# Delta-rule heads: both quarters of filling of a level in front of its second product

## What is computed

```python
lower = jnp.where(strict, jnp.einsum("bhncd,bhnsd->bhncs", k_beta, k) * decay, 0.0)
t_inv = lax.linalg.triangular_solve(eye + lower, jnp.broadcast_to(eye, lower.shape),
                                    left_side=True, lower=True, unit_diagonal=True)
u = jnp.einsum("bhncs,bhnse->bhnce", t_inv, v_beta)
w = jnp.einsum("bhncs,bhnsd->bhncd", t_inv, k_beta * eg[..., None])
def step(state, xs):
    q_c, qk_c, u_c, w_c, k_c, gl = xs
    v_new = u_c - jnp.einsum("bhcd,bhde->bhce", w_c, state)
    o = jnp.einsum("bhcd,bhde->bhce", q_c, state) + jnp.einsum("bhcs,bhse->bhce", qk_c, v_new)
    state = state * jnp.exp(gl)[..., None, None] + jnp.einsum("bhcd,bhce->bhde", k_c, v_new)
    return state, o
```

## Time and profile before

| | |
|---|---|
| median of 3 runs | 2359.76 us (2343.94 to 2362.39) |
| profiled execution | 2355.82 us, span 2354.1 us |
| TensorE busy | 2219.3 us, 94% of the span |
| VectorE, ScalarE, GpSimd busy | 57%, 36%, 24% |
| chain that ended last | TensorE 75%, VectorE 15%, issue 4%, ScalarE 2%, DMA 2% |
| heads 0 to 7 | about 100 to 720 us, 78.3 to 78.4 us for each of the heads in the middle |

### The profile page before, as it was taken

One profiled execution on the slowest core, in us unless ns is written; L12 is line 12 of the kernel. 1 busy time (PEld: TensorE's weight loads), 2 busy tenths in 40 slices (PEclk: granted clock), 3 DMA queues, 4 the chain that ended last, 5 costly groups with the idle time before them and its releaser, 6 DMA issues.

```text
span 2354.1 us, 31041 instructions
## 1 busy us (share of the span) xinstructions
PE 2219.3 (94%) x10792; PEld 1831.5 (78%) x10792; DVE 1335.0 (57%) x1845; ACT 847.9 (36%) x1239; POOL 561.8 (24%) x584
## 2 busy tenths in 40 slices
PE   5899999999979999999999999999899999999997
PEld 5687878787867877888888788888666677888886
DVE  6667656765663445343356655554577776655531
ACT  1323222322222223223223545432456554554422
POOL 3277667766770012000011000001000000000021
PEclk6899999999999999999999999999999999999999
DMA  6233333333322322333333233333211112333332
GB/s 223 81 99 90 92 94 98 91 92 94 98 81 72 98 87 84 98 96 92 93 95 99 80 98 98 98 90 98 63 54 54 52 48 86 101 98 98 92 92 67
DMA packets 355154, 212.78 MB, mean 90 GB/s; under 512 B 8536, under 2 KB 342802, under 8 KB 354963
## 3 DMA queue, kind: packets, MB, share of 16 engines
q1 hardware_dynamic: 346346, 185.82, 27.1%
q0 software_dynamic: 7680, 25.17, 3.5%
q10 hardware_dynamic: 1065, 0.96, 0.1%
HBM read 209.82 MB, written 2.10 MB: 90 GB/s over the span
## 4 chain that ended last, share of the span: by engine, by line
PE 75%; DVE 15%; issue 4%; ACT 2%; DMA 2%; DVEq 0%; ACTq 0%; POOL 0%; POOLq 0%; SPq 0%
PE ps L1970 22%; PE ps L1972 22%; PE ps L1971 22%; PE ps L2140 3%; PE ps L1997 2%; DVE w_lo L1155 2%; DMA raw<-diff_w_qkv 1%; DVE small L1854 1%; DVE small L1485 1%; DVE gd_y_t L1459 1%; DVE a_sb L1883 1%; DVE gd_q_s L1346 1%; ACT at_swap L1059 1%; DVE gd_q_g L1447 1%; PE ps L2089 1%
## 5 line engine op out<-in xcount | busy, mean ns | idle before, releaser
L1970 PE MATMUL ps<-h_hi,w_hi 128*128 128x512 f32 x1896 | 776.3, 409 | 33.8 <-DVE gd_y_t L1459 8.9
L1972 PE MATMUL ps<-h_hi,w_lo 128*128 128x512 f32 x1896 | 750.7, 396 | 0.0
L1971 PE MATMUL ps<-h_lo,w_hi 128*128 128x512 f32 x1896 | 750.1, 396 | 0.0
L1155 DVE TENSOR_TENSOR w_lo<-raw,w_hi 128x1024 fp32r<-128x1024 f32 x336 | 442.6, 1318 | 417.3 <-ACT w_hi L691 416.6
L691 ACT ACTIVATE w_hi<-raw 128x1024 fp32r<-128x1024 f32 x336 | 355.6, 1059 | 746.1 <-PE ps L1972 676.9
L1970 PEld LDWEIGHTS ps<-h_hi,w_hi 128*128 128x128 f32 x1896 | 363.5, 192 | 114.5 <-issue 39.0
L1972 PEld LDWEIGHTS ps<-h_hi,w_lo 128*128 128x128 f32 x1896 | 362.6, 191 | 79.6
L1971 PEld LDWEIGHTS ps<-h_lo,w_hi 128*128 128x128 f32 x1896 | 363.8, 192 | 67.2
L561 POOL TENSOR_TENSOR sq_sum<-x 128x512 f32<-128x512 f32 x5 | 5.2, 1040 | 913.2 <-DVE x L1681 488.6
L1970 PE MATMUL ps<-act_hi,w_hi 128*128 128x512 f32 x528 | 206.6, 391 | 0.0
L1971 PE MATMUL ps<-act_lo,w_hi 128*128 128x512 f32 x528 | 206.1, 390 | 0.0
(11 more groups left out here) (345 smaller groups left out, 2895.0 us busy)
## 6 DMA issues: line engine op xcount, KB each, us to landing
raw<-ffn_w_up SPq DMA_DIRECT2D x88, 512.0 KB, 3.8
raw<-w_in SPq DMA_DIRECT2D x72, 512.0 KB, 3.8
raw<-w_ffn_in SPq DMA_DIRECT2D x44, 512.0 KB, 3.8
ada_w<-w_ada POOLq DMA_DIRECT2D x64, 256.0 KB, 3.4
raw<-ffn_w_down SPq DMA_DIRECT2D x32, 512.0 KB, 3.6
raw<-diff_w_qkv SPq DMA_DIRECT2D x24, 512.0 KB, 3.8
ada<-w_ada SPq DMA_DIRECT2D x4, 2048.0 KB, 15.7
ada_w<-w_ada_f POOLq DMA_DIRECT2D x32, 256.0 KB, 3.2
```

The lines of the kernel that those rows point to most:

```text
L1155: nc.vector.tensor_tensor(w_lo[:, tile.slot], raw[:, tile.raw], w_hi[:, tile.slot].bitcast(F32), SUB)\
L1970: nc.tensor.matmul(dst, w_hi[:, tile.slot, k], hi, start=first, stop=False)
L1971: nc.tensor.matmul(dst, w_hi[:, tile.slot, k], lo, start=False, stop=False)
L1972: return nc.tensor.matmul(dst, w_lo[:, tile.slot, k], hi, start=False, stop=last)
```

## The change

Only the table `HEAD_FILL` changes, so only heads 0 to 6. The number of quarters stays 32.

```diff
-HEAD_FILL = {name: 1 for name in PE_STEPS if name != "w" and name not in [f"u{_n}" for _n in range(LEVELS - 1)]}
-HEAD_FILL.update(kb_rows=2, x_pairs=3, o_sums=2, o_norm_rows=2)
+HEAD_FILL = {name: 2 for name in ["kb_rows", "kk_qk", "u5", "o_sums", "o_norm_rows"] + [f"x{_n}" for _n in range(LEVELS - 1)]}
+HEAD_FILL.update({f"{name}{_n}": 1 for name in ("v_new", "o") for _n in range(NC)}, kv_tokens=1, x_pairs=3)
```

## The result

| | before | after |
|---|---|---|
| median | 2359.12 us (2343.94 to 2362.39, 4 runs) | 2377.11 us (2376.25 to 2380.74, 4 runs) |
| profiled execution's span | 2354.1 us | 2376.2 us |
| TensorE busy | 2219.3 us | 2219.9 us |
| VectorE, GpSimd busy | 1335.0, 561.8 us | 1353.2, 568.4 us |
| one head of the loop (heads 1 to 5) | 78.3 to 78.4 us | 79.6 to 82.0 us |

The changed kernel is slower by 0.94% (ratio 1.0094, 95% interval 1.0073 to 1.0116). I had forecast 2370 us, 10 us more than before; it became 18 us more. The time lies in the range and within 1%, but the cost is nearly double of what the sum gave. The heads in the middle, but for head 2, lie above the 81 us that I had named as a sign of being wrong.

A forecast was written before the change was run, and what follows sets the result against it. TensorE, busy 94% of the span, was taken as the bound. Level 5 at 1.4 us over 7 heads gave 9.8 us on the 2359.8 us median, forecast 2370 us, range 2353 to 2383; g_rows counted 0.

The forecast's parts named there:

- the 81 us: Loop heads should last 79.8 us, not 78.4; above 81 would show the forecast wrong, by clock or late splits.
- the place and the sign at level 5: At level 5 both quarters stand behind the y5 copy wait, so u5 comes 1.4 us later per head.
- The level price of 5.59 us: One level costs 5.59 us instead of 5.43, since 0.16 us between x product and next y is not hidden.
- the wait for L888: At y0, TensorE newly waits about 0.9 us for ScalarE's copy of the x_pairs transposes.
- the late x1 copy: At level 1 VectorE's x copy is late behind L1485, so y2 starts about 207.8, not 207.24.
- the wait ends where it ended: At level 5 the y5 copy wait ends as before, so u5's quarters start at 227.47, independent of TensorE.
- the long split: VectorE's weight split before the y5 copy takes 2.42 us, as in six of seven heads, instead of 1.22.
- rival 1: Short splits before the y5 copy: loss only 0.4 us per head, 3 us in all, 2363 us; chance 0.15.
- g_rows at 0: Moving one quarter from g_rows to kk_qk costs and gains nothing, since kb_rows stands behind as many quarters.
- GpSimd's order of work does not move: Reason for 1.4 us per head at the level 5 split; spread 0.4 to 2.6 if splits change sides.
- everything behind u5 shifts with it: After u5, a TensorE chain with fillings as before comes 1.4 us later, with no further cost.
- Rival 4: A gap at y5 drops the clock to 1.2 GHz, slowing quarters and products: 32 us, 2391 us; chance 0.07.

The follow-up runs named there:

- the kernel with the levels alone: Changed kernel with g_rows and kk_qk back at 1 and 1, so only the levels are changed: 2380.3 us, ratio 1.0094.
- short GpSimd: GpSimd's modulation multiply and first sum on 32 of 128 columns, result not the reference's: 2353.6 us on the changed kernel, 2336.5 us on the kernel before.
- g_rows alone: Kernel before with only g_rows' quarter moved to kk_qk (0 and 2), levels unchanged: 2359.6 us, ratio 1.0007.
- the version that beats both: Kernel before with u5's quarter put before the wait for the y5 copy and kk_qk's quarter moved to kv_tokens: 2337.6 us, ratio 0.9899.
- the changed kernel with x5: Changed kernel with both quarters of u5 put in front of the wait for the y5 copy: 2359.2 us, ratio 1.0005.

## Why the prediction was right and wrong

**Right: the place and the sign at level 5.** Two quarters behind the wait for the y5 copy and nothing in front of it cost time, and moving them in front of the wait took all of the measured loss back. The level price of 5.59 us, the wait for L888 and the late x1 copy came out to 0.1 us.

**Wrong, and near by luck: "the wait ends where it ended".** I let the long split end the wait for the y5 copy, as head 3 of the kernel with the levels alone does. In the changed kernel the split is short in all seven heads, and y5 itself is late in six of them. VectorE, head 1:

```profile
231.27 1.22 DVE L1155 TENSOR_TENSOR w_lo<-raw,w_hi 128x1024 fp32r<-128x1024 f32 x1
232.60 0.69 DVE L1459 TENSOR_TENSOR gd_y_t<-ps,cst 128x512 f32<-128x512 f32 x1
```

What ends the wait now is the way from the y5 product (231.41) over its copy to the quarter (233.42), 2.0 us. The short GpSimd shows the same way with y5 in time: quarters at 31.8, u5 at 34.6, 0.4 us behind the kernel before, which is the price of rival 1. So my quarters (32.8) lie only 0.5 us from the measured ones (33.31) because a lateness that I had not seen stands in the place of a split that I had taken for long. The 1.9 us that u5 is late are 0.97 for y5 and 1.37 for the second quarter behind the wait, less the 0.44 by which the way from y5 to the quarters got shorter.

**Wrong: g_rows at 0.** I asked what the earlier rows release, and kb_rows indeed gives nothing back. I did not ask what the rows wait for. In front of the transposes stands a wait for VectorE's L1416, and the moved quarter had been its cover. It costs 1.1 us per head, 7 us, in the trace. My own list of waits could not show it, because it was hidden.

**Wrong: "GpSimd's order of work does not move".** It did not, but VectorE's did, by up to 0.7 us, and a VectorE instruction that had stood in a gap of GpSimd fell behind a DMA issue. I had weighed this for one instruction, the split of level 4. There it went the good way: the split is 1.22 us long and not 2.42. What I did not weigh is that another of VectorE's instructions with two inputs in SBUF can be the one. It was L1354, which took 2.8 us more than alone.

**Wrong: "everything behind u5 shifts with it".** From w to the norm the changed kernel needs 21.6 us in heads 3 to 5, and 19.8 before. The first and the third o product wait for VectorE's copy of v_new, 1.13 and 0.50 us. VectorE reaches these copies behind a short convolution and weight splits, which come 2 us later than before and collide with GpSimd. This is the changed kernel, VectorE, head 3; before, the same taps (x2) took 1.89 us, the first split 1.22 and the second 1.44.

```profile
399.81 3.23 DVE L1394 SCALAR_TENSOR_TENSOR gd_cc<-gd_th,vec,gd_cc 128x511 f32<-128x511 f32 x2
402.96 1.76 DVE L1155 TENSOR_TENSOR w_lo<-raw,w_hi 128x1024 fp32r<-128x1024 f32 x1
404.64 0.28 DVE L1508 COPY gd_y_t<-ps 128x128 f32<-128x128 f32 x1
...
410.48 2.56 DVE L1155 TENSOR_TENSOR w_lo<-raw,w_hi 128x1024 fp32r<-128x1024 f32 x1
```

```profile
404.97 0.49 PE L2196 MATMUL ps<-gd_qk_t,gd_y_t 128*128 128x128 f32 x2 [1.13 <-DVE gd_y_t L1508]
...
413.30 0.49 PE L2195 MATMUL ps<-gd_q_g,state 128*128 128x128 f32 x2 [0.50 <-DVE gd_y_t L1508]
```

That these rows are collisions is supported by the short GpSimd, with which this stretch is as long in the changed order (36.4 to 55.85, 19.4 us) as in the order before (35.1 to 54.5, 19.4 us). Together with L1354 it is, as I read it, the 9 or 10 us by which the two pairs differ.

**Rival 4, the clock, was half right.** In two heads the gap at y5 is followed by a fall, and u5's quarters take 233.42 to 237.86, 4.44 us, as I had priced it. The further 1.6 us for the products u5 and w did not come: from one to the other it is 1.80 us in head 1, with the fall, and in head 3, without. Nor was the idle time in front of the quarters longer than before, 0.86 against 1.41 us. The other heads have the same gap and no fall, and the loop has two falls fewer in all than before. I took the falls in the norm for a fixed part of a head. They are not. So the clock made the changed kernel faster than its waits, not slower. The Trainium skill (TensorE: Matmul & The Clock Gate, HAM oscillation — how this bites in real kernels) warns that gaps between bursts of matmuls bring the clock down. Here the gap by itself does not decide it: heads 1 and 3 have the same 2.0 us from the y5 product to the quarters behind it, one with a fall and one without.

The sum of a head without a fall, in heads 3 to 5: 81.7 against 76.8, 4.9 us. It is 1.9 up to u5 (forecast 1.4), 1.8 from w to the norm (forecast 0), 1.1 at g_rows (forecast 0). The fall of 1.6 us that these heads no longer have leaves 3.3 us. So two terms that I had put at 0 are most of what the sum lacked.

## What to carry to other kernels

When filling work moves away from a place, look at the instruction that stood behind it and at everything it waits for, also those waits that the profile doesn't show, since they were covered. Put filling between the producing product and the wait for its copy; a filling that stands behind the wait does not cover it. Both quarters moved from behind that wait to in front of it won back 18 us in the changed kernel, and the one quarter 6 us in the kernel before. Compare two orders by the waits and by the granted clock separately: a new wait of 1.1 us per head came, in the profiled execution, with four falls of the clock fewer, and its cost could not be seen in the time.

## What I had not expected of the hardware

- A VectorE instruction that reads two operands in SBUF can end only behind several GpSimd instructions: L1354 began at 224.21 inside a DMA issue (224.05 to 224.84), and ended at 227.71, behind a mask and a multiply that followed each other without a gap. The Trainium skill (SBUF — State Buffer, Who interferes with whom) says that whichever issues first has the shared ports for the whole instruction, and that the other is blocked. Here the end came only behind three. It ends 0.56 us behind the end of the multiply, where GpSimd pauses for 0.08 us. It also began 0.65 us ahead of the mask, and still waited for it, which this rule by itself does not give.
- Whether it waits hangs on hundredths of a microsecond. In the four kernels that have the changed levels and the full GpSimd, the activation took 3.49 to 3.54 us in the 21 heads in which it began 0.12 to 0.17 us behind the start of the DMA issue, and 0.68 us in the three in which it began 0.10 to 0.12 us behind it and in the four in which it began ahead of it. This is one of the three, from the kernel with the levels alone:

```profile
383.47 0.68 DVE L1355 SCALAR_TENSOR_TENSOR gd_k_s<-gd_th,gd_k_s 128x512 f32<-128x512 f32 x1
```

```profile
383.35 0.79 POOL L599 DMA_DIRECT2D ada_w<-w_ada  x1 [0.64 <-POOL ada_s L606]
```

With the short GpSimd it begins within 0.01 us of the issue in six heads and 0.15 us ahead of it in one, and takes 0.68 us in all. So that pair takes the collision away, but it does not tell whether GpSimd's shorter work or the earlier start does it.
- The DMA issue by itself does not hold VectorE. In the kernel before with the short GpSimd, a split with two inputs in SBUF begins 0.37 us behind the start of an issue that no GpSimd instruction follows for 1.83 us, and takes its usual 1.22 us:

```profile
207.00 1.22 DVE L1155 TENSOR_TENSOR w_lo<-raw,w_hi 128x1024 fp32r<-128x1024 f32 x1
```

```profile
206.63 0.79 POOL L598 DMA_DIRECT2D ada_w<-w_ada  x1 [0.64 <-POOL ada_s L605]
```

So I take it that the instructions behind the issue hold L1354; why they do so although it began ahead of them stays open.
- The granted clock may or may not fall at the same instructions. The norm's one-column matmuls are the same in every kernel; behind them the clock fell in six of seven heads of the kernel before, in two with g_rows alone and in none of the version that beats both. Nor is it the length of the head: heads 3 to 5 last 78.4 us in the kernel before, each with a fall, and 78.4 us in the changed kernel with x5, without one. What decides it was not tested.
